# Output weights in exchanged ring places, and split operands laid out buffer by buffer, in a two-layer MoE decoder kernel

## What is computed

```python
z = h @ w_in + b_in                                   # 1024 -> 8448 columns
merged = (gates[0] * (oa @ w_proj_a) + gates[1] * (ob @ w_proj_b)
          + gates[2] * (oc @ w_proj_c))
x = x + merged @ w_out                                # 1024 x 1024
t = rms_norm(x, g2)                                   # router and experts read this
hg = einsum("nd,edf->nef", t, w_gate)                 # 32 experts, 1024 x 256 each
hu = einsum("nd,edf->nef", t, w_up)
y  = einsum("nef,efd->nd", silu(hg) * hu * combine, w_down)
x = x + y
```

## Time and profile before

| | |
|---|---|
| median of 3 runs | 1022.11 us (1021.55 to 1023.45) |
| the profiled execution, its own time | 1022.55 us |
| its span, first to last instruction | 1020.6 us |
| TensorE (PE) busy | 959.6 us, 94% |
| VectorE (DVE) busy | 560.0 us, 55% |
| ScalarE (ACT) busy | 430.6 us, 42% |
| moved by DMA | 313.03 MB, mean 307 GB/s |
| granted TensorE clock, mean | 0.98 of full speed |

### The profile page before, as it was taken

One profiled execution on the slowest core, in us unless ns is written; L12 is line 12 of the kernel. 1 busy time (PEld: TensorE's weight loads), 2 busy tenths in 40 slices (PEclk: granted clock), 3 DMA queues, 4 the chain that ended last, 5 costly groups with the idle time before them and its releaser, 6 DMA issues.

```text
span 1020.6 us, 15602 instructions
## 1 busy us (share of the span) xinstructions
PE 959.6 (94%) x5906; PEld 671.5 (66%) x5906; DVE 560.0 (55%) x1320; ACT 430.6 (42%) x918; POOL 58.4 (6%) x74
## 2 busy tenths in 40 slices
PE   9999999999999995986999999999999999977877
PEld 7888877788886441542588888777888954344323
DVE  7666787786873332220276668787869534122212
ACT  5434566766444110210354355676764441111122
POOL 1120400000010000000004004000000100000000
PEclk9999999999999998997999999999999999989899
DMA  9975633247999999999997765332589999999996
GB/s 348 348 249 185 202 126 125 83 130 274 407 358 403 427 426 423 425 427 427 418 400 242 235 185 186 124 124 83 171 307 385 362 425 427 425 424 424 427 427 276
DMA packets 97114, 313.03 MB, mean 307 GB/s; under 512 B 13424, under 2 KB 18576, under 8 KB 74512
## 3 DMA queue, kind: packets, MB, share of 16 engines
q1 hardware_dynamic: 96704, 312.04, 79.7%
q10 hardware_dynamic: 336, 0.02, 0.0%
HBM read 310.20 MB, written 1.84 MB: 306 GB/s over the span
## 4 chain that ended last, share of the span: by engine, by line
PE 78%; DMA 11%; SPq 7%; DVE 2%; ACT 1%; issue 1%; POOL 0%; DVEq 0%; POOLq 0%; ACTq 0%
PE ps L1451 16%; PE ps L1453 15%; PE ps L1452 15%; SPq L491 7%; PE ps L2079 6%; DMA arena<-in_w_expert_gate_dram 5%; DMA arena<-in_w_expert_up_dram 5%; PE ps L2053 2%; PE ps L1574 2%; PE ps L1476 2%; PE ps L2153 2%; PE ps L2165 2%; PE ps L1586 2%; PE ps L2024 1%; PE ps L2106 1%; PE ps L1602 1%
## 5 line engine op out<-in xcount | busy, mean ns | idle before, releaser
L1103 DVE TENSOR_TENSOR wlo<-arena,whi 128x512 fp32r<-128x512 f32 (+1 forms) x352 | 233.1, 701 | 101.8 <-ACT whi L896 98.7
L1451 PE MATMUL ps<-whi,ahi 128*128 128x512 f32 (+1 forms) x736 | 284.3, 386 | 0.1
L1453 PE MATMUL ps<-whi,alo 128*128 128x512 f32 (+1 forms) x736 | 277.1, 376 | 0.0
L1452 PE MATMUL ps<-wlo,ahi 128*128 128x512 f32 (+1 forms) x736 | 276.9, 376 | 0.0
L896 ACT CAST whi<-arena 128x1024 fp32r<-128x1024 f32 (+1 forms) x171 | 175.8, 1031 | 177.6 <-PE ps L1453 170.9
L1451 PEld LDWEIGHTS ps<-whi,ahi 128*128 128x128 f32 x736 | 138.5, 188 | 27.7 <-issue 3.3
L1453 PEld LDWEIGHTS ps<-whi,alo 128*128 128x128 f32 x736 | 138.4, 188 | 26.0
L1452 PEld LDWEIGHTS ps<-wlo,ahi 128*128 128x128 f32 x736 | 138.7, 189 | 23.1
L2308 DVE SCALAR_TENSOR_TENSOR acts<-ps,wslot,acts 128x256 f32<-128x256 f32 x16 | 7.7, 484 | 169.8 <-ACT acts L1980 146.4
L2079 PE MATMUL ps<-arena,rows 128*32 128x512 f32 x416 | 92.0, 628 | 6.7 <-DMA arena<-in_w_expert_up_dram 5.5
L2079 PE MATMUL ps<-ring_rest,rows 128*32 128x512 f32 x352 | 77.9, 643 | 11.9 <-DMA arena<-in_w_expert_up_dram 11.9
(11 more groups left out here) (295 smaller groups left out, 1078.1 us busy)
## 6 DMA issues: line engine op xcount, KB each, us to landing
arena<-in_w_in_dram SPq DMA_DIRECT2D x62, 1024.0 KB, 5.3
arena<-in_w_expert_down_dram SPq DMA_DIRECT2D x36, 1024.0 KB, 19.7
arena<-in_w_expert_gate_dram SPq DMA_DIRECT2D x34, 1024.0 KB, 24.9
arena<-in_w_expert_up_dram SPq DMA_DIRECT2D x32, 1024.0 KB, 24.4
ring_rest<-in_w_expert_down_dram SPq DMA_DIRECT2D x24, 1024.0 KB, 18.1
ring_rest<-in_w_expert_gate_dram SPq DMA_DIRECT2D x22, 1024.0 KB, 24.5
ring_rest<-in_w_expert_up_dram SPq DMA_DIRECT2D x22, 1024.0 KB, 25.7
arena<-in_w_proj_a_dram SPq DMA_DIRECT2D x8, 1024.0 KB, 5.0
```

The source lines that it names most:

```text
L1103: dve.tensor_tensor(wlo[:, jj % 2, cols], half_slot(jj, w)[:, cols], whi[:, jj % 2, cols].bitcast(F32), ALU.subtract).then_inc(low_split i ...
L1451: pe.matmul(o, hi, rhs_hi, start=first, stop=False)
L1452: pe.matmul(o, hi, rhs_lo, start=False, stop=False)
L1453: return pe.matmul(o, lo, rhs_hi, start=False, stop=last)
```

## The change

Three things are done together.

1. `whi` and `wlo` become views of one tile in which each buffer's high and low part lie side by side; `ahi` and `alo` likewise by groups of four blocks. Slot 12 then lies over buffer 0, 13 over buffer 1, 14 to 17 over the block groups 0-3, 4-7, 8-11 and 12-15. Slots 14 and 15 come free once blocks 0 to 7 are done, 12 and 16 after half 90, 13 and 17 after the last half.
2. The quarters of `w_out` exchange places: r = 2 and 3 are loaded first, in places 2 and 3, r = 0 and 1 after them, in places 0 and 1. The order in which they are used stays. Slots 8, 9, 10 and 11 then come free one by one.
3. SyncE's order changes with this: slots 5, 2, 6 and 4, which went out before or between items 42 to 44, now follow the third and fourth `w_out` load. `squares_act` waits for quarters 2 and 3 too before its first square, since quarter 0 now goes to a PSUM bank.

```diff
+        split_w = sb("split_w", [P, 2, 2, SLOT // 2], F32R)
+        whi, wlo = split_w[:, :, 0, :], split_w[:, :, 1, :]
+        split_a = sb("split_a", [P, 4, 2, 4, S], F32R)
+        def a_block(part, k):
+            return split_a[:, k // 4, part, k % 4, :]
...
-        JUNK = tuple(ps[:, 1 + q, :] if q in (1, 2) else arena[:, RING_A * SLOT:] for q in range(4))
+        JUNK = (ps[:, 3, :], ps[:, 2, :], ps[:, 3, :], arena[:, RING_A * SLOT:])
...
-            act.wait_ge(x_done, 4 * nh + 2)
+            act.wait_ge(x_done, 4 * nh + (2 if nh else 4))
...
-                        + [("out", r) for r in range(4)])
+                        + [("out", r) for r in (2, 3, 0, 1)])
+                def seat(item):
+                    return {42: 44, 43: 45, 44: 42, 45: 43}.get(item, item)
+                def ring_at(item):
+                    return seat(item) % RING
...
                             if item == 39:
                                 sp.wait_ge(obt_ready, 3)
                                 sp.wait_ge(o_lo, 5)
-                                load_ahead(0, 1, 5)
-                            if item == 42:
+                                load_ahead(0, 1)
+                            if item == 44:
+                                load_ahead(5)
                                 sp.wait_ge(gated, 4)
-                                load_ahead(2, 6)
-                            if item == 43:
+                                load_ahead(2)
+                            if item == 45:
+                                load_ahead(6)
                                 sp.wait_ge(gated, 8)
                                 load_ahead(4)
                         sp.wait_ge(gates_ready, 3)
...
                         sp.wait_ge(quarter_ready, 12)
-                        load_ahead(14, 16)
+                        load_ahead(14, 15)
+                        sp.wait_ge(low_split, 2 * 43)
+                        load_ahead(8)
                         sp.wait_ge(low_split, 2 * 44)
+                        load_ahead(9)
+                        sp.wait_ge(low_split, NARROW + 3)
+                        load_ahead(10)
+                        sp.wait_ge(low_split, NARROW + 4)
                         load_ahead(11)
-                        sp.wait_ge(low_split, NARROW + 3)
-                        load_ahead(8)
-                        sp.wait_ge(low_split, NARROW + 4)
-                        load_ahead(9, 10)
+                        item_used(sp, NARROW + 2)
+                        load_ahead(12, 16)
...
-                    if PLACES[i] in (12, 13, 15, 17):
+                    if PLACES[i] in (13, 17):
                         load(sp, i + 2, False)
```

More of the change, by code:

```diff
@@ L177, in trunk_program, with a_pair @@
             y_lo = sb("y_lo", [P, D], F32R, ctx)
[L179 to L182, removed]
+        split_w = sb("split_w", [P, 2, 2, SLOT // 2], F32R)
+        whi, wlo = split_w[:, :, 0, :], split_w[:, :, 1, :]
+        HI, LO = 0, 1
+        split_a = sb("split_a", [P, 4, 2, 4, S], F32R)
+        def a_block(part, k):
+            return split_a[:, k // 4, part, k % 4, :]
+        def a_pair(part, k):
+            return split_a[:, k // 4, part, k % 4:k % 4 + 2, :]
         wst = sb("wst", [P, B_GROUPS, P])
@@ L639, in halved_blocks, with ring_landed @@
                     return ((w_proj_b[l], r, 4, r // 2, 0),)
-                def ring_landed(slot, item):
-                    return 16 * (item // 4 + 1 + (slot == 0 and item >= 40))
+                def ring_landed(item):
+                    at = seat(item)
+                    return 16 * (at // 4 + 1 + (at % RING == 0 and at >= 40))
                 def heads(b):
@@ L859, in split_at @@
                         kb = 8 + 2 * i if i < 4 else 0
-                        return t[:, kb:kb + 2, :].rearrange("p k (t c) -> p k t c", t=TB)
+                        return a_pair(t, kb).rearrange("p k (t c) -> p k t c", t=TB)
                     def narrow_slot(j, kk):
                         c, item = divmod(j - NARROW, 2)
-                        blocks = ring[:, (NARROW // 2 + item) % RING, :].rearrange("p (k n) -> p k n", k=4)
+                        blocks = ring[:, ring_at(NARROW // 2 + item), :].rearrange("p (k n) -> p k n", k=4)
                         ks = slice(2 * kk, 2 * kk + 2) if kk is not None else slice(0, 4)
@@ L871, in half_slot @@
                         n = 2 * w
-                        return ring[:, (j // 2) % RING, (j % 2) * n:(j % 2) * n + n]
+                        return ring[:, ring_at(j // 2), (j % 2) * n:(j % 2) * n + n]
                     @block.scalar
@@ L886, in high @@
                             if landed is not None:
-                                act.wait_ge(ring_in[(jj // 2) % RING], landed)
+                                act.wait_ge(ring_in[ring_at(jj // 2)], landed)
                             if used is not None:
@@ L947, in high_at @@
                                 item = NARROW // 2 + j % 2
-                                act.wait_ge(ring_in[item % RING], ring_landed(item % RING, item))
+                                act.wait_ge(ring_in[ring_at(item)], ring_landed(item))
                                 high(j, BANK, None, None)
                                 return
-                            high(j, TAIL if 64 <= j < Z_CONV else BANK, ring_landed(j // 2 % RING, j // 2), j - 1 if j < 64 else None)
+                            high(j, TAIL if 64 <= j < Z_CONV else BANK, ring_landed(j // 2), j - 1 if j < 64 else None)
                         for j in range(32, 40):
@@ L1475, in both @@
                                 for tb in range(TB):
-                                    mm = pe.matmul(ps[:, tb, :], part[:, kb, tb * P:(tb + 1) * P],
+                                    mm = pe.matmul(ps[:, tb, :], a_block(part, kb)[:, tb * P:(tb + 1) * P],
                                                    w_part[:, j % 2, kk * BANK:(kk + 1) * BANK],
-                                                   start=kb == 0 and part is ahi and w_part is whi,
+                                                   start=kb == 0 and part == HI and w_part is whi,
                                                    stop=kb == KB - 1 and w_part is wlo)
```

36 lines of the change are left out of this document (17 added, 19 removed).

## The result

The changed kernel takes 1027.64 us (median of 6 runs, 1026.53 to 1028.22); the kernel before, with three runs more than those of the first table, 1023.31 (6 runs, 1021.55 to 1024.13). The ratio is 1.0044, 95% interval 1.0034 to 1.0054: slower by 4.3 us. The forecast was 1027.9, and slower. The profiled execution took 1027.5, its span is 1025.5.

A forecast was written before the change was run, and what follows sets the result against it. The prediction took the queue of transfers, not TensorE, to bound the expert stage. Two layers at +2.9 us gave +5.8 on the profiled 1022.55, so 1028.35, or 1027.9 against the median; range 1024.1 to 1030.9.

The forecast's parts named there:

- What bounds the kernel: Expert stage: bound by the transfer queue, not TensorE; each microsecond of empty queue before 313 costs one at the layer's end.
- The front pauses: In 263 to 276 of layer 1, the queue stands empty for about 1.0, 2.9 and 2.9 us.
- Rival 1: Front and back of the load stretch cancel, at 3.6 us of front pause; time 1022, within 2 us; chance 0.09.
- Data 1.75 us after an issue into an empty queue: Front: a load issued into an empty queue has data flowing 1.75 us later, read off the lone `w_proj_c` load.
- Rival 4: Front: data flow 1.0 us after an issue, not 1.75; +2.2 us a layer, 1026.5 us; chance 0.10.
- All holes behind 276 close: Rest of the stretch, from 276: the queue stays full, closing today's holes of 0.6 + 1.1 + 0.6 + 1.3 = 3.6 us.
- The sum of +2.9 us a layer: Per layer, the estimated delay from front pauses less closed holes: 2.9 us, with bounds +1.0 and +4.4.
- Four are first parts: Among the stretch's last twenty loads, slots 2, 3, `first_slot` and 11 were taken at 2.95 us each.
- The last byte of the 29: End of the 29-load stretch (30.4 MB): through at 327.1 instead of 324.1 us in layer 1, 6 us later in layer 2.
- What costs nothing: Trunk: new layouts, later first square and late fourth `w_out` load (TensorE standing 1 to 2 us near 290) add zero.
- Rival 3: Near 290: the late fourth `w_out` load stalls TensorE unhidden by the queue; +1.5 us a layer, 1030.9 us; chance 0.07.
- Rival 2: Closed holes of 301 to 313 are full gain, the front not empty; 7.2 us faster, 1014.9 us; chance 0.09.

The follow-up runs named there:

- run 6: Changed kernel with slot 2 and its `gated` wait moved behind the fourth `w_out` load; 1030.32 us against 1022.87 for the kernel before, ratio 1.0073.
- run 3: Kernel before with only the new split-tile layout and the slots it frees; 1021.49 us against 1023.06 for the kernel before, ratio 0.9977.
- run 1: Kernel before with only the change's order of early loads in the front; 1027.67 us against 1023.06 for the kernel before, ratio 1.0039.
- run 5: Changed kernel with slot 5 alone issued early again, behind item 39; 1025.40 us against 1022.87 for the kernel before, ratio 1.0025.
- run 2: Changed kernel with slots 5, 2 and 6 issued early again, slot 4 behind the third `w_out` load; 1024.46 us against 1023.06 before, ratio 1.001.
- run 8: The kernel of run 3 measured again with more runs; 1020.72 us (median of 12) against 1022.87 for the kernel before, ratio 0.998.
- run 7: Changed kernel with all four `load_ahead` lines of the front as before; 1031.78 us against 1022.87 for the kernel before, ratio 1.009.

## Why the prediction was right

- **What bounds the kernel**: right. Only the time at which bytes are through moved the end, and run 6, with TensorE's stall gone and the queue's pauses longer, is the slowest but one.
- **The front pauses** of about 1.0, 2.9 and 2.9 us: right. 267 to 270 moves 38 GB/s and 273 to 276 moves 69. At 426 GB/s their 6 us miss 2.2 MB or 5.2 us of flow; the second pause begins already in 272 to 273 (213 GB/s), which makes it some 5.7, and 5.8 were forecast for these two. The window of 263 to 276 was forecast near 210, and it is 190. Rival 1 needed 3.6 us of pause and falls. Its argument has a slip: what lies between the issues at 268.60 and 274.05 is 5.45 us; 5.8 is the sum of two pauses.
- **Data 1.75 us after an issue into an empty queue**: right. The second `w_out` load was issued at 268.2, and its 3 us from 270 move 330 GB/s, 0.99 MB, nearly all of the load. Read off windows of 1 us it is 1.7 to 1.8 us in each pause. Rival 4, a flow from 1.0 us on, falls. Yet something does move by then, which explains the share of 1.01 in the earlier trace rows: cut finer, the first bytes show at 269.25, 1.0 us after the issue's start, in a burst of some 50 KB in 0.3 us (171 GB/s over 269.22 to 269.52), and behind it 25 GB/s over 0.5 us until the flow begins near 270. The second pause is alike: issued at 273.67, first bytes at 274.70. The Trainium skill, "DMA: Bandwidth & Descriptors", section Specifications, gives about 0.6 us to the first byte of a load issued by the sync engine. The trace agrees if that is counted from the end of the issue (268.22 + 0.37, so 0.66 us); the flow, by which the forecast goes, begins 1.1 us later still.
- **All holes behind 276 close**: right but for 282 to 284, at 229 and 260 GB/s, and 310 to 313 at 400. From 313 to 440, stretches of 11 us and longer move 424 to 429.
- **The sum of +2.9 us a layer**: the one term that was mis-sized; it is +2.3. The step is "Four are first parts. For these I take the window of 283 to 301": 2.95 us each. In the changed kernel the same window moves 411 GB/s instead of 389. By the windows of the kernel before I had taken a stretch with small holes of its own for the price of the loads in it. If the bytes of the 1 us windows are counted off in the order of issue, slots 3, `first_slot` and 11 take 2.6, 2.5 and 2.6 us in the changed kernel, and slot 2, in the dip of 282 to 284, takes 3.4: 11.1 us for the four instead of 11.8. The other 16 loads take 39.5, as forecast. This counting is an estimate, since neighbouring transfers can overlap.
- **The last byte of the 29**: through at 326.1 us instead of 324.1 in layer 1 (3 later forecast; counted from slot 18's issue it is 2.3) and at 832.7 instead of 827.3 in layer 2 (6 forecast). TensorE's waits for weights in the experts of layer 1 (390 to 500) grow from 8.0 to 12.2 us, as forecast. The window of 766 to 779 that the forecast named reads 281 GB/s, because layer 2's slot 18 goes out 2.9 us later here; its own front is the 188 shown above.
- **What costs nothing**: right. ScalarE came late and TensorE stood for 0.6 us in layer 1 and 1.5 us in layer 2 (1 to 2 forecast), and the queue hid it: the 73 loads behind take 180.0 us with the stall (the change) and 179.9 without it (run 6). Rival 3 falls with it. The layout costs nothing in the instructions either. VectorE's low splits between 242 and 313, before and after (the first fence is the kernel before, the second the changed one; count, then busy us and mean ns):

```profile
L1103 DVE TENSOR_TENSOR wlo<-arena,whi 128x512 fp32r<-128x512 f32 x34 | 22.0, 688 | 9.1 <-ACT whi L896 8.7
```

```profile
L1122 DVE TENSOR_TENSOR split_w<-arena,split_w 128x512 fp32r<-128x512 f32 x34 | 22.0, 688 | 9.1 <-ACT split_w L915 8.7
```

- **Rival 2**, that closed holes are a gain, has a part that is true, though not in this change: with a full front, run 3 closes the hole of 310 to 313 and gains. What I had not seen is the upper end of such a gain. I wrote "from 313 on every load stands behind another"; that holds for the kernel before, for the change and for runs 1, 5 and 6. Those whose 29 loads are through earlier (runs 2, 3 and 8) run dry near 347, where the next slots come free by TensorE's work and not by the queue's, and so does run 7 near 352, its TensorE being late. Runs 3 and 8 gain 0.5 to 1.2 us a layer. That not much more could be had from the queue without TensorE being earlier as well, and that the 7.2 us of that rival were out of reach, is argued from these holes; no run has tried it.

That the size came out so near has a share of luck: the sum of two layers is 4.6, the measured difference 4.3, the forecast 5.8, on a median of the kernel before that itself moved from 1022.11 to 1023.31 when three runs were added to its three.

## What to carry to other kernels

In a stretch that ends behind a full queue of loads, count empty time in the queue from the first load that can be sent early, and not waits of engines: a hole closed at the back gains nothing if it is filled by bytes taken from the front. Whatever can be issued early should go ahead of the loads that wait for an engine, except ahead of one that an engine will soon need (run 7 lost 8.9 us that way). A change of several parts should be timed part by part: here the layout alone was worth -2 us and the front's issue order alone +4.6. Their prices don't add up: all three parts together cost 4.3 and not 2.6, since with an empty front the hole that the layout would fill is full already (run 1, with the old layout, moves 429 GB/s in 310 to 313).

## What the runs showed of the hardware

- From SyncE's issue into an empty queue until data flow steadily it takes 1.7 to 1.8 us here, in each of the pauses; a burst of some 50 KB comes 1.0 us after the issue. A load issued right as the queue runs empty is thus 1.7 us too late. What the burst is, no run shows.
- A stretch of loads that stand behind each other moves the same bytes in the same time: 76.5 MB in 179.8 to 180.0 us in all twelve layers of six profiles (before, the change twice, runs 1, 5 and 6), whatever went ahead. Small differences of a kernel of 1023 us can so be found in one profile, where the span itself varies by 1 us.
- The price of 512 KB transfers with 2 KB runs read from a stretch that isn't quite full is too high: 389 GB/s there, 411 with more loads behind them; by the estimate above a pair takes 2.5 to 2.6 us in a full queue and not 2.95.
- A stall of 3.0 us costs TensorE more than 3.0 us: in run 7 the granted clock fell to 0.50 behind it for some 3 us. Behind the changed kernel's stall of 0.6 us the clock stayed at 1.00 in all windows shown.
- What stays open: why 310 to 313 of the changed kernel stays at 400 GB/s and why 282 to 284 dips, and by how much run 7's two losses (TensorE's late end, SyncE's late issues) add up each by itself. No run takes them apart.
